# The 5-tap convolution of the gated scan's input stage moved from VectorE to GpSimd

## What is computed

```
qkv, z, ab, glu = jnp.split(h @ w_in, EVEN_SPLITS, axis=-1)
qkv = jax.nn.silu(depthwise_conv(qkv, qkv_conv))          # 5 taps, 1536 channels
...
val, gate = jnp.split(glu, 2, axis=-1)
y = depthwise_conv(val * jax.nn.sigmoid(gate), dw_conv) + dw_bias   # 31 taps, 512 channels
```

## Time and profile before

| what | value |
|---|---|
| median of 3 runs | 3732.95 us (3732.86 to 3736.82) |
| the profiled execution's own time | 3728.49 us |
| its span | 3726.7 us |
| mean granted TensorE clock | 0.937 |
| TensorE matmul busy | 3396.4 us, 91% |
| VectorE busy | 1470.8 us, 39% |
| ScalarE busy | 877.2 us, 24% |
| GpSimd busy | 10.8 us |

### The profile page before, as it was taken

How to read it: one execution, slowest core, us unless ns; L and a number is a source line. 1 busy time by engine, 2 the same in 40 slices (tenths; PEclk the granted TensorE clock), 3 DMA queues, 4 the chain that set the end, 5 groups by cost and what they waited for, 6 DMA issues and landing times.

```text
span 3726.7 us, 44964 instructions
## 1 busy us (share of the span) xinstructions
PE 3396.4 (91%) x18812; PEld 2745.5 (74%) x18812; DVE 1470.8 (39%) x2480; ACT 877.2 (24%) x1374; POOL 10.8 (0%) x35
## 2 busy tenths in 40 slices
PE   7879999987899998999898887889998999975898
PEld 6669987676798876888544587648886788854798
DVE  0635410225362104333286566533333434315454
ACT  2224200122331003222202111222222222121333
POOL 0000000000000000000000000000000000000000
PEclk9889999998899999999898798799999999987899
DMA  5415588543256883222312200312222222210252
GB/s 215 170 47 192 192 285 287 196 152 159 81 183 244 287 282 123 98 94 101 113 67 94 79 23 23 114 68 96 96 100 81 79 95 97 79 68 0 102 181 102
DMA packets 69101, 479.41 MB, mean 129 GB/s; under 512 B 7360, under 2 KB 10816, under 8 KB 11712
## 3 DMA queue, kind: packets, MB, share of 16 engines
q1 hardware_dynamic: 67600, 473.09, 36.0%
q10 hardware_dynamic: 1328, 3.85, 0.3%
HBM read 475.87 MB, written 1.05 MB: 128 GB/s over the span
## 4 chain that ended last, share of the span: by engine, by line
PE 70%; DVE 9%; PEld 8%; issue 5%; ACT 4%; PEldq 3%; DMA 1%; ACTq 1%; DVEq 0%; SPq 0%
PE ps L502 15%; PE ps L510 14%; PE ps L512 14%; PE ps L511 14%; PEld ps L502 7%; PE ps L1284 4%; PE ps L746 1%; PE ps L1413 1%; ACT X L769 1%; PE ps L1715 1%; PE ps L841 1%; PE ps L1421 1%; PE ps L1731 1%; ACT area L764 1%; PE ps L1296 1%
## 5 line engine op out<-in xcount | busy, mean ns | idle before, releaser
L531 DVE TENSOR_TENSOR w_lo<-ring,w_hi 128x1024 fp32r<-128x1024 f32 x360 | 439.0, 1223 | 636.9 <-ACT w_hi L523 636.9
L523 ACT ACTIVATE w_hi<-ring 128x1024 fp32r<-128x1024 f32 x360 | 378.5, 1056 | 763.4 <-PE ps L512 648.6
L510 PE MATMUL ps<-x_hi,w_hi 128*128 128x512 f32 (+1 forms) x1408 | 516.3, 367 | 44.2 <-DVE x_lo L650 42.4
L511 PE MATMUL ps<-x_lo,w_hi 128*128 128x512 f32 (+1 forms) x1408 | 514.1, 365 | 0.0
L512 PE MATMUL ps<-x_hi,w_lo 128*128 128x512 f32 (+1 forms) x1408 | 513.8, 365 | 0.0
L502 PEld LDWEIGHTS ps<-area,ring 128*128 128x128 f32 x3240 | 383.3, 193 | 46.3 <-issue 41.0
L502 PE MATMUL ps<-area,ring 128*128 128x128 f32 (+4 forms) x3240 | 405.5, 286 | 1.6 <-DVEq L800 1.6
L510 PEld LDWEIGHTS ps<-x_hi,w_hi 128*128 128x128 f32 x1408 | 268.0, 190 | 94.0 <-issue 43.5
L502 PE MATMUL ps<-HM,ring 128*128 128x256 f32 (+1 forms) x928 | 297.7, 483 | 19.7 <-DVEq L800 14.8
L512 PEld LDWEIGHTS ps<-x_hi,w_lo 128*128 128x128 f32 x1408 | 268.3, 191 | 42.0
L511 PEld LDWEIGHTS ps<-x_lo,w_hi 128*128 128x128 f32 x1408 | 268.5, 191 | 40.4
(11 more groups left out here) (360 smaller groups left out, 4337.7 us busy)
## 6 DMA issues: line engine op xcount, KB each, us to landing
ring<-in_moe_up SPq DMA_DIRECT2D x128, 1024.0 KB, 4.9
ring<-in_ff_up SPq DMA_DIRECT2D x88, 1024.0 KB, 4.8
ring<-in_ada SPq DMA_DIRECT2D x72, 1024.0 KB, 5.4
ring<-in_moe_down SPq DMA_DIRECT2D x64, 1024.0 KB, 4.9
ring<-in_ff_down SPq DMA_DIRECT2D x44, 1024.0 KB, 4.8
ring<-in_w_in SPq DMA_DIRECT2D x14, 1024.0 KB, 6.2
ring<-in_even_in SPq DMA_DIRECT2D x10, 1024.0 KB, 4.9
ring<-in_w_o SPq DMA_DIRECT2D x8, 1024.0 KB, 5.3
```

The source lines that it names most:

```text
L510: pe.matmul(dst, hi, xh, start=start, stop=False, skip_group_check=True)
L511: pe.matmul(dst, hi, xl, start=False, stop=False, skip_group_check=True)
L523: act.activation(w_hi[:, j % HALVES, :], ring[:, u % SLOTS, (j % 2) * D:(j % 2 + 1) * D], ACT.Copy)\
L531: dve.tensor_tensor(w_lo[:, j % HALVES, :], ring[:, u % SLOTS, (j % 2) * D:(j % 2 + 1) * D], w_hi[:, j % HALVES, :].bitcast(F32), ALU.subt ...
```

## The change

The borders of `CI` and the 5-tap convolution leave VectorE's program and go into a new one for GpSimd, `in2_pool`, which is called from `modulation_pool` just before the site `b2.0.conv_end`. A fused multiply-add becomes two GpSimd instructions, a product into one of two halves of the scratch buffer `row` and an addition into `QKV`. ScalarE's Silus wait on a new semaphore `pool_conv`. The 31-tap convolution stays on VectorE.

```diff
-                           dve=["g0", "g1", "g2", "g3"] + [f"conv{c}" for c in range(12)])
+                           dve=["g0", "g1", "g2", "g3"])
...
+                if key == "b2.0.conv_end":
+                    in2_pool(pool, "b2.0.in")
...
-                act.wait_ge(dve_done, st.v("dve", f"conv{c}"))
+                act.wait_ge(pool_conv, c + 1)
...
+            dve.drain().then_inc(dve_done, 1)
+
+        def in2_pool(pool, n):
+            st = enter(pool, n)
+            pool_link = Chain(pool, pool_step)
+            hc = GCONV // 2
+            pool.memset(CI[:, :, :, 0:hc].rearrange("p a b c -> p (a b) c"), 0.0)
+            pool_link(pool.memset(CI[:, :, :, hc + T:].rearrange("p a b c -> p (a b) c"), 0.0))
             for c in range(12):
                 o = seqs(QKV[:, c, :])
-                dve.wait_ge(act_done, st.v("act", f"c{c + 8}"))
-                link(dve.tensor_scalar(o, CI[:, c, :, 0:T], col("gconv", c * GCONV), None, ALU.mult))
+                pool.wait_ge(act_done, st.v("act", f"c{c + 8}"))
+                pool_link(pool.tensor_scalar(o, CI[:, c, :, 0:T], col("gconv", c * GCONV), None, ALU.mult))
                 for k in range(1, GCONV):
-                    ins = dve.scalar_tensor_tensor(o, CI[:, c, :, k:k + T], col("gconv", c * GCONV + k), o, ALU.mult, ALU.add)
+                    part_ = seqs(row[:, k % 2, :])
+                    pool_link(pool.tensor_scalar(part_, CI[:, c, :, k:k + T], col("gconv", c * GCONV + k), None, ALU.mult))
+                    ins = pool.tensor_tensor(o, o, part_, ALU.add)
                     if k < GCONV - 1:
-                        link(ins)
-                ins.then_inc(dve_done, st.one("dve", f"conv{c}"))
-            dve.drain().then_inc(dve_done, 1)
+                        pool_link(ins)
+                ins.then_inc(pool_conv, 1)
```

More of the change, by code:

```diff
@@ L195, in build @@
         act_step, dve_step = sem("act_step"), sem("dve_step")
+        pool_step, pool_conv = sem("pool_step"), sem("pool_conv")
         arrived = [sem(f"arrived{i}") for i in range(SLOTS)]
@@ L1529, in in2_dve @@
             st = enter(dve, n)
-            hc, hl = GCONV // 2, CCONV // 2
-            dve.memset(CI[:, :, :, 0:hc].rearrange("p a b c -> p (a b) c"), 0.0)
-            dve.memset(CI[:, :, :, hc + T:].rearrange("p a b c -> p (a b) c"), 0.0)
+            hl = CCONV // 2
             dve.memset(GL[:, :, :, 0:hl].rearrange("p a b c -> p (a b) c"), 0.0)
```

## The result

The median went from 3733.56 to 3802.36 us (3794.51 to 3803.36, 4 runs each); the ratio to the kernel before is 1.0178, with a 95% interval of 1.016 to 1.0196. By that ratio the change costs 66.5 us, with an interval of 60 to 73; the difference of the two medians is 68.8. The forecast was 3769 within 3742 to 3803: the direction and the place were right, and the size was short by some 30 us. The result lies less than 1 us inside the upper end of the whole range, and outside the forecast's own range of 3755 to 3785.

A forecast was written before the change was run, and what follows sets the result against it. TensorE's `z` was taken to bound the stage, with GpSimd ending it after the change: 33.8 us plus 2.6 for the clock, 36.4 on 3728.5, gives 3764.9, or 3769 against the median; own range 3755 to 3785, whole range 3742 to 3803.

The forecast's parts named there:

- The bound of the stage: Convolution stage: TensorE ends it with `z`; VectorE is early by 6.9 us, so taking 42.7 us off VectorE is worth nothing.
- limit of 9.48 us a block: Most that GpSimd may take per block of the 5-tap convolution for the last Silu to end before TensorE's `z`.
- GpSimd's product: Each of 60 scalings of 512 columns in the 5-tap convolution on GpSimd: 0.65 us alone, bounds 547 to 1370 ns.
- The addition: Each of 48 additions of 512 columns in the 5-tap convolution on GpSimd: 1.33 us alone, from 1.0 to 1.6.
- The waits: Between two chained GpSimd instructions of the 5-tap convolution: 0.1 us for each of nine in a block.
- The two engines' holding: GpSimd and VectorE alternate during the 31-tap convolution: 81 turns of 1.47 us, 119 us; VectorE's convolution ends 55 us later.
- The pause on TensorE: TensorE idles some 36 us before the mean's product, which then runs at a lower clock: 2.6 us charged.
- It all hides: Rival: no holding either way and a block at no more than 9.48 us; 3733 to 3740 us, 12 in 100.
- GpSimd is held, VectorE is not: Rival: beside the 31-tap convolution only GpSimd waits, 0.24 us each; stage +11.4 us, time 3747, 12 in 100.
- VectorE always wins: Rival: GpSimd may not get in until the 31-tap convolution ends at 1969.73; stage +64.1 us, time 3800, 12 in 100.
- Alternating, but dearer: Rival: nothing of the two engines overlaps, 1.80 us a turn, or products take 1.0 us; time 3796, 10 in 100.
- Faster: Rival: full clock after a pause, in 2045 to 2061, gives up to 8 us back; 3725 us, 3 in 100.

## Why the prediction was right or wrong

**The bound of the stage** was read rightly: nothing that leaves VectorE shortens it. The kernel with the borders alone and the one with three blocks moved show it. The limit of 9.48 us a block, 113.8 for twelve, holds in every kernel that leaves the whole convolution to GpSimd. Where GpSimd took less, the stage stayed as it was; where it took more, the stage grew by the excess (us; GpSimd from its first product's start to its last instruction's end):

| kernel | GpSimd, twelve blocks | above 113.8 | stage longer by |
|---|---|---|---|
| additions left out | 108.5 | none | 0.4 |
| narrow instructions | 119.1 | 5.3 | 5.6 |
| products of two tensors | 157.6 | 43.8 | 44.0 |
| VectorE's chain cut away | 162.8 | 49.0 | 49.4 |
| a constant as the factor | 172.0 | 58.2 | 58.5 |
| the change | 177.2 | 63.4 | 63.7 |

**GpSimd's product is the step that failed.** The forecast took 0.65 us, between 0.55 and 1.37, "near" the copy of 256 columns because both read and write one tensor. It is 1.56 us, outside the bounds. The 0.59 ns a column came from a line between two different operations, a scaling of 16 columns and a copy of 256, and the copy is no guide to the scaling: at 256 columns it takes 0.40 us where the scaling takes 0.93, and the scaling's own slope is 2.5 ns. Why a scaling is so dear, and dearer than a multiplication of two tensors, no run shows. The high bound, built with the slope of the additions, was 0.19 us too low. Sixty products make 60 x 0.91 = 54.6 us of error.

**The addition** was forecast at 1.33 and is 1.26: the small rows from 16 to 32 columns extrapolated to within 6%, 3.4 us in all. The slope stood on 36 ns between 16 and 32 columns, in a trace that also has additions of 8 columns at 0.25 to 0.30 us, slower than those of 16; it was the narrow instructions that bore it out. The prediction's other estimate, 1.12 us, lay further off. **The waits** of 0.1 us were right. A block alone is 13.57 us instead of 9.47.

**The two engines' holding** was right in kind and too dear in size. The forecast let them take turns strictly, 1.47 us a turn, which put 34 us on top of GpSimd's own 113.6. The runs show 14.3 us on top of 162.8. The assumption that failed is that GpSimd's instruction keeps VectorE out for all but its last 0.15 us. An addition lengthens a multiply-add by 1.64 - 0.75 = 0.89 us, but a product by 0.31 only, and VectorE's next one passes beside the same product untouched. VectorE's 31-tap convolution ended 2008.06 - 1849.36 = 158.7 us into the stage, 30.2 us later than before, where 55 were forecast.

So +49.2 us on GpSimd's price and -19.7 on the holding make +29.5 of the 29.9 by which the stage, at +63.7 instead of +33.8, missed the forecast. The two errors partly cancelled, and that is luck: with the holding as dear as forecast the time would have been near 3822 us, above the whole range.

**The rule of the Trainium skill's page "SBUF — State Buffer", section "Who interferes with whom"**, is that a multiply-add with two SBUF inputs and a GpSimd instruction that reads SBUF contend, and that the lock between them is exclusive. The trace agrees that they hold each other. It does not agree that one stands fully blocked while the other runs, as the prediction read the rule: a product of 1.88 us holds VectorE for 0.31, and the next multiply-add beside it not at all. The measurement decides.

**The pause on TensorE** was charged with 2.6 us, and no run shows such a price. The mean's product takes 6.17 us instead of 3.67. But it takes 5.35 after a wait of 2.05 us and 5.34 after one of 60.24, at a granted clock of 0.68 in both:

```profile
2018.96 5.35 PE L503 MATMUL ps<-area,cons 128*128 128x512 f32 x8 [2.05 <-ACTq L1528]
2085.29 5.34 PE L503 MATMUL ps<-area,cons 128*128 128x512 f32 x8 [60.24 <-ACTq L1528]
```

The first is of the kernel with the borders alone, the second of the one with a constant factor. The 3.67 us of the earlier trace rows, at a clock of 1.00, is the odd one: the same product after the same wait takes 5.35 to 5.37 in three other kernels. What lies behind the stage takes 1704.7 us in the kernel before, 1706.5 in the changed one, and 1704.8 to 1707.2 in the eight others, without an order by the length of the wait (1704.8 after 60.24 us, 1706.5 after 7.35). So the 1.8 us can't be told from the spread of single executions.

**The rivals.** "It all hides" is refuted for the change as made, and true once the blocks cost 9.04 us on average. "GpSimd is held, VectorE is not" and "VectorE always wins" fall with the multiply-adds of 1.64 us and with the 52 GpSimd instructions finished beside them. "Alternating, but dearer" named products of 1.0 us as a way to 3796. It had the right culprit and was given 10 in 100. "Faster" falls with the time; the granted clock was 0.50 again, in 2117 to 2133 of the changed kernel, the stretch that corresponds to 2045 to 2061.

## What to carry to other kernels

Ask first whether the engine to be relieved ends the stage, and how much time the new one has until something else ends it: here 9.48 us a block on average, and everything above it was paid twelve times. Price an elementwise instruction on GpSimd from the same operation at two widths; another operation with the same number of operands misled by more than a factor of two. Work moved to GpSimd beside a chain of VectorE instructions with two SBUF inputs slows that chain too: with a quarter of the blocks moved, VectorE ended later than with none.

## What the runs showed that was not expected

- On GpSimd, a scaling of 128x512 took 1.56 us (1.49 with a constant), an addition of two tensors 1.26, and a multiplication by a broadcast column 1.04. The instruction with one tensor input was the slowest of the three.
- Beside an addition on GpSimd, VectorE's multiply-add of 0.75 us took 1.64; at the start of a scaling 1.06; in the rest of the scaling 0.75; beside a multiplication by a broadcast column 1.41.
